# Work at the seams between head pairs moved, and VectorE's remainders ahead of its biased scores

## The reference, cut to what matters

```python
q, k, v = (c.reshape(bsz, seq, 8, 64) for c in (c_q, c_k, c_v))
logf = log_sigmoid(c_f + b_forget);  cum = cumsum(logf, axis=1)
for i in range(8):                        # blocks of 128 queries
    s = q[block i] @ k[:end].T * scale + cum[block i] - cum[:end]   # causal
    p = softmax(s);  o[block i] = p @ v[:end]
y_c = (o * silu(c_gate)) @ p_c
y_m = (softmax(m_q @ mk.T * scale) @ mv * silu(m_gate)) @ p_m
merged = sum_i sigmoid(g_i) * y_i         # i = A, B, C, M
x = layer_norm(alpha * x + merged @ w_out)
```

## Time and profile before

| | us |
|---|---|
| median of 3 runs | 1241.01 (1240.44 to 1241.07) |
| the profiled execution's own time | 1239.63 |
| its span | 1237.8 |
| TensorE busy | 1207.7 (98%) |
| VectorE busy | 800.5 (65%) |
| ScalarE busy | 538.4 (43%) |
| POOL busy | 636.5 (51%) |

### The profile page before, as it was taken

The page is one execution under the profiler, slowest core; times in us unless marked ns, Lnnn a source line. Parts: engine busy times, 40 slices in busy tenths (PEclk is TensorE's granted clock), DMA queues, the critical chain, the costliest instruction groups (busy, mean ns, idle before and its releaser), DMA issues.

```text
span 1237.8 us, 16499 instructions
## 1 busy us (share of the span) xinstructions
PE 1207.7 (98%) x5704; PEld 999.1 (81%) x5704; DVE 800.5 (65%) x1318; ACT 538.4 (43%) x991; POOL 636.5 (51%) x518
## 2 busy tenths in 40 slices
PE   8999999999999999999999999999999999999997
PEld 6888888888888888888788878778787888778886
DVE  5623865676665855347696766677666786876755
ACT  5433424344434444565354555545555443415000
POOL 6687787877876877867122322323312225547000
PEclk9999999999999999999999999999999999999999
DMA  8022131132232332336221111111002533377231
GB/s 274 2 67 69 34 102 51 67 122 104 101 136 102 102 125 86 130 104 200 73 69 52 35 34 51 34 51 51 18 18 86 177 121 115 107 238 249 66 136 68
DMA packets 91268, 118.49 MB, mean 96 GB/s; under 512 B 6072, under 2 KB 72632, under 8 KB 91200
## 3 DMA queue, kind: packets, MB, share of 16 engines
q1 hardware_dynamic: 91200, 117.60, 29.0%
HBM read 92.39 MB, written 25.20 MB: 95 GB/s over the span
## 4 chain that ended last, share of the span: by engine, by line
PE 85%; DVE 8%; issue 3%; ACT 2%; POOL 1%; DMA 1%; DVEq 0%; SPq 0%; ACTq 0%; POOLq 0%
PE pj L744 11%; PE pj L746 11%; PE pj L745 11%; PE pj L816 4%; PE pj L815 4%; PE pj L817 4%; PE pj L1067 4%; PE pt L746 3%; PE pt L744 3%; PE pt L745 3%; PE po L928 2%; PE pj L832 2%; PE pj L834 2%; PE pj L833 2%; PE pt L915 2%
## 5 line engine op out<-in xcount | busy, mean ns | idle before, releaser
L1560 POOL TENSOR_TENSOR ring_lo<-w_pair,ring_hi 128x512 fp32r<-128x512 f32 x168 | 232.3, 1385 | 112.1 <-ACT ring_hi L1123 111.9
L1613 POOL TENSOR_TENSOR w_lo<-w_raw,w_hi 128x128 fp32r<-128x128 f32 (+1 forms) x104 | 108.7, 1063 | 215.1 <-ACT w_hi L1213 213.0
L1123 ACT ACTIVATE ring_hi<-w_pair 128x512 fp32r<-128x512 f32 x168 | 105.1, 628 | 160.6 <-PE pj L746 108.6
L1756 DVE SCALAR_TENSOR_TENSOR po<-glu,cwa,po 128x512 f32<-128x512 f32 x232 | 159.5, 749 | 20.6 <-ACT po L1174 20.6
L744 PE MATMUL pj<-t_hi,ring_hi 128*128 128x512 f32 x392 | 152.8, 390 | 0.3 <-DVE slot L1720 0.3
L746 PE MATMUL pj<-t_hi,ring_lo 128*128 128x512 f32 x392 | 152.5, 389 | 0.0
L745 PE MATMUL pj<-t_lo,ring_hi 128*128 128x512 f32 x392 | 152.5, 389 | 0.0
L815 PE MATMUL pj<-xT_hi,w_hi 128*128 128x512 f32 x320 | 126.4, 395 | 0.0
L816 PE MATMUL pj<-xT_lo,w_hi 128*128 128x512 f32 x320 | 125.5, 392 | 0.0
L817 PE MATMUL pj<-xT_hi,w_lo 128*128 128x512 f32 x320 | 125.0, 391 | 0.0
L1720 DVE TENSOR_TENSOR slot<-pj,copy_p 128x512 f32<-128x512 f32 x56 | 38.6, 689 | 85.6 <-PE pj L746 85.4
(11 more groups left out here) (343 smaller groups left out, 2927.8 us busy)
## 6 DMA issues: line engine op xcount, KB each, us to landing
w_pair<-in_w_in SPq DMA_DIRECT2D x28, 1024.0 KB, 5.2
gate_scratch<-slot SPq DMA_DIRECT2D x16, 1024.0 KB, 4.0
gate<-gate_scratch SPq DMA_DIRECT2D x32, 512.0 KB, 3.7
w_raw<-in_w_in SPq DMA_DIRECT2D x20, 512.0 KB, 3.9
z_scratch<-slot SPq DMA_DIRECT2D x8, 512.0 KB, 2.6
bias<-cum_scratch SPq DMA_DIRECT2D x8, 512.0 KB, 3.7
wout_raw<-in_w_out SPq DMA_DIRECT2D x8, 512.0 KB, 6.2
x_tok<-in_x SPq DMA_DIRECT2D x8, 512.0 KB, 4.2
```

The lines of the kernel that those rows point to most:

```text
L1123: nc.scalar.activation(ring_hi[:, j % RING, :, :], w_src(u, p), ACT.Copy).then_inc(s_rhi, 1)
L1560: nc.gpsimd.tensor_tensor(ring_lo[:, j % RING, :, :], w_src(u, p), ring_hi[:, j % RING, :, :], ALU.subtract).then_inc(s_rlo, 1)
L1613: nc.gpsimd.tensor_tensor(w_lo[:, j % 2, k, :], w_raw[:, j % 2, k, :], w_hi[:, j % 2, k, :], ALU.subtract).then_inc(s_wlo, 1)
L1756: nc.vector.scalar_tensor_tensor(out=acc if n < PAD_A else src, in0=src, scalar=cwa[:, ct, n:n + 1], in1=acc, op0=ALU.mult, op1=ALU.add).t ...
```

## The change

Four edits, none of which changes what is computed.

1. TensorE: the last weighing of a pair (`weigh(c, 7)`) moves behind the first part of the stream in unit 0 of the next pair, and for the last pair behind the first `m_fill` of the memory part. `turn_v` moves from the head of a pair to unit 1, behind the stream's first part, with the two banks of `pt` in swapped order. The last memory weighing moves behind the first half tile of the projection of C. The turning of `mem` is done in two halves with half a tile of stream between them.
2. ScalarE, VectorE and POOL: their counterparts follow. The move and addition of the last output half stand in iteration 1 of the next pair; the copy and remainder of v stand there too, behind `exp` on ScalarE and `biased` on VectorE; POOL's product of z stands in iteration 2, behind the mask addition.
3. VectorE: in each iteration k, `turned_lo(c, k - 1)` stands ahead of `biased(c, k + 1)`, where it was behind it.
4. The four loops over pairs (TensorE, ScalarE, POOL, VectorE) and the one of SP are written out, and three semaphore increments that nobody waits for are gone.

```diff
@@ tensor: weighing, turning of v
-                if n >= 2:
+                if c or n >= 2:
                     pe.wait_ge(s_oadd, PV_PAIR * c + n - 1)
...
-                pe.wait_ge(s_pjfree, 8 * c + 6)
+                pe.wait_ge(s_pjfree, 8 * c + 4 if c else 6)
                 for b in range(2):
+                    if c or b:
+                        pe.wait_ge(s_tlo, TB_PAIR * c + b)
...
             def pair(c, last):
                 s = 4 * c
-                turn_v(c)
                 for u in range(UNITS):
                     cut = 4 * u + (3 if u == 0 else 2)
                     stream_part(s + S_C, S_C, 4 * u, cut)
+                    if u == 0 and c:
+                        weigh(c - 1, UNITS // 2 - 1)
+                    if u == 1:
+                        turn_v(c)
                     turn(c, u)
                     if u + 2 < UNITS or not last:
                         scores(c, u + 2)
                     stream_part(s + S_C, S_C, cut, 4 * u + 4)
                     if u % 2 == 0 and u:
                         weigh(c, u // 2 - 1)
-                weigh(c, UNITS // 2 - 1)
...
+            turn_mem(0)
             pe.wait_ge(s_xfree[1], NP // 2 - 1)
-            stream_tile(1, 1, back=None, halves=range(1, 2))
-            pe.wait_ge(s_mte, n)
+            k_steps(1, 1, 1, 0, KT // 2, 3)
+            turn_mem(1)
+            k_steps(1, 1, 1, KT // 2, KT, 3)
+            pe.wait_ge(s_mte, 2 * MT)
...
             for w in range(2 * NT):
                 m_fill(PER * w, PER * w + 5)
+                if w == 0:
+                    weigh(CT - 1, UNITS // 2 - 1)
...
-            mweigh(NT - 1)
-
             for s in range(S_P + IN_M, S_END):
...
                     p_steps(s, h, 0, p_k(s), 2 * ((s + 1) % 2) + h)
+                    if s == S_P + IN_M and h == 0:
+                        mweigh(NT - 1)
@@ scalar
                 for k in range(UNITS):
+                    if k == 1 and c:
+                        out_shift(1, UNITS // 2 - 1, PV_PAIR * c - 1)
                     if k:
                         turned_hi(c, k - 1)
                         if k + 1 < UNITS or not last:
                             exp(c, k + 1)
+                    if k == 1:
+                        for b in range(2):
+                            act.wait_ge(s_tb, TB_PAIR * c + b + 2)
+                            nc.scalar.activation(v_stack[...], pt[:, 1 - b, :]..., ACT.Copy).then_inc(s_thi, 1)
@@ gpsimd
+                    if k == 2 and c:
+                        z_product(c - 1)
@@ vector
                 if u >= 2:
-                    dve.wait_ge(s_tb, tb + tb_before(u - 1))
+                    dve.wait_ge(s_tb, tb + tb_done(u - 2))
...
                 for k in range(1, UNITS):
+                    turned_lo(c, k - 1)
                     if k + 1 < UNITS or not last:
                         biased(c, k + 1)
-                    turned_lo(c, k - 1)
+                    if k == 1:
+                        for b in range(2):
+                            dve.wait_ge(s_thi, TB_PAIR * c + b + 2)
+                            nc.vector.tensor_tensor(v_stack[...], pt[:, 1 - b, :]..., ...).then_inc(s_tlo, 1)
                     if k + 1 < UNITS or not last:
                         normalise(c, k + 1)
+                    if k == 1 and c:
+                        out_add(1, UNITS // 2 - 1, zc(UNITS // 2 - 1, c - 1), PV_PAIR * c - 1)
...
             mmax(0)
             mnormalise(0)
+            out_add(1, UNITS // 2 - 1, z_raw[:, CT - 1, T - 2 * P:T], PV - 1)
@@ all five engines
-            with pe.Fori(0, CT - 1) as c:
-                pair(c, False)
-            pair(CT - 1, True)
+            for c in range(CT):
+                pair(c, c == CT - 1)
```

## The result

The changed kernel takes 1268.68 us (median of 6 runs, 1267.22 to 1269.64), the kernel before, beside it on the same chip, 1240.57 (6 runs). The ratio is 1.0225, 95% interval 1.0214 to 1.0236: 28.1 us slower, where 1267 was forecast. The profiled execution took 1267.22 us with a span of 1265.4; before it was 1239.63 and 1237.8. It is the fastest of the six, at a mean granted clock of 0.996 where the other five show 0.994 or 0.995.

A forecast was written before the change was run, and what follows sets the result against it. TensorE was taken to bound the kernel. VectorE's order (+34.6 us), the seams (-8.9) and the turning of mem (+0.4) summed to +26.1, said as 1267 us for the median, with an 8 in 10 range of 1248 to 1280.

The forecast's parts named there:

- VectorE's order: In the four pairs: remainder ahead of biased scores makes TensorE's scores wait, 34.6 us slower, bounds 17 to 44.
- odd units: In each pair: remainder plus biased scores end after TensorE wants the banks, 4.3 us lost per pair.
- The removed counters: Semaphore increments taken out, together with the loops written out: priced at 0.
- Units 1 and 2: Where v is turned: late transposes of unit 1 (0.35) and scores of unit 4 (0.75), 1.1 us per pair.
- Even units: In each pair, without units 1 and 2: VectorE comes late from the odd iteration before, 3.5 us lost per pair.
- The seams: Between pairs and around the memory part: moved steps cover TensorE's waits, 8.9 us gained, bounds 6.6 and 9.8.
- the moved weighing: Last pair's end and memory part: stream steps and this weighing cover TensorE's waits, 1.9 of 2.2 us gained.
- The turning of `mem`: Ahead of the first scores: two halves with stream steps between, net 0.4 us slower, bounds -0.7 and +1.1.
- (a): Rival: the order on VectorE costs nothing and only the seams count, 1232 us, chance 0.06.
- (b): Rival: only the odd units pay, as VectorE catches up in the even ones, 1249 us, chance 0.12.
- (d): Rival: the gains and losses cancel, 1241 us, chance 0.02.
- (c): Rival: more stalls than counted, from POOL's product beside VectorE and from written-out code, 1276 us at most, chance 0.14.

The follow-up runs named there:

- e1: The changed kernel with VectorE's old order again, biased scores of unit k+1 ahead of the remainder of unit k-1: 1236.65 us.
- e4: The changed kernel, with VectorE taking the remainder first only in even iterations k and the biased scores first in odd ones: 1238.66 us.
- e8: The changed kernel with the weighing of each even unit directly behind the scores, ahead of the second part of the stream: 1246.92 us.
- e9: The changed kernel with two increments that nobody waits for put back in front of VectorE's two biased-score instructions: 1276.17 us.
- e5: The changed kernel with the first weight split of a pair, on ScalarE and POOL, moved behind the copies of v in iteration 1: 1266.92 us.
- e7: e1 with the last pair's last weighing, its move and addition back where they were, ahead of the memory part: 1235.26 us.
- e2: The kernel before with its five loops over pairs written out and nothing else: 1241.18 us.
- e6: e1 with the turning of mem in one go, as before the change: 1235.10 us.

## Why the prediction was right, and where it was off

**VectorE's order.** Right in its mechanism, and near in its size: 31.3 us measured, 34.6 forecast. e1, e4 and e8 show it from three sides: the cost goes with the order (32.0), with the odd iterations (30.0 of these), and in part, about 14, with an earlier weighing. The odd units came to 3.7 us a pair where 4.3 was forecast, and unit 5, forecast at 1.11, to 0.92; units 11 and 13 came to 1.09 and 0.70 where 0.87 and 0.9 stood. The looped pair spans 83.4 us, as forecast. Of the other signs, the stall at the seam's weighing is gone, and the wait for the biased scores is there, 26 times in the list, six or seven a pair where twelve were named; ten of a pair's units from 3 on are later by over 0.1 us. The longest are units 11 (1.09) and 5 (0.92), not 5 and 13.

**The removed counters.** Priced at 0, which failed. In the changed kernel their absence saves 7.5 us (e9), as it shortens the biased scores by 0.15 us in a unit; I had taken those from the earlier trace rows with the gap inside them. With the counters in place the terms that I put under the order would have come to some 39 us, an estimate (31.3 and 7.5), where 34.6 stood. That the measured 31.3 is near the forecast is in part luck: 34.6 was too low for biased scores with the gap inside, and their getting shorter hid it.

**Units 1 and 2.** The step that failed by its size: 1.1 forecast, 2.6 measured. I had put the stall at unit 1's transposes at 0.35 and it is 2.28. I followed the remainder of v behind the biased scores and the exponential of unit 2, but not those behind the copy `pT_hi` of unit 0, which stands behind a k half (1.06) and two weight splits (1.16) on ScalarE. In the old order VectorE ran the biased scores ahead of that remainder, and in the new one it waits with them. Half of the stall isn't the order's at all: e1, with the old order, has 1.15 in every pair, and the first pair has no more than that in the changed kernel either. e5 shows that this list makes the stall, and also that undoing it alone gives nothing back.

**Even units.** 3.5 forecast without units 1 and 2, 2.4 measured. Unit 4 came to 0.07 where +0.4 stood, unit 6 to 0.25 and unit 8 to 0.35 where 0.65 and 0.6 stood. Units 12 and 14 came to 0.90 and 0.52 where 1.2 and 0.65 stood, but unit 10, put at 0, to 0.29. e9 shows the counters' part: with them back, each of these units is 0.15 later. That leaves 0.1 to 0.25 in each of the others, and 0.44 the other way in unit 10, without an explanation.

**The seams.** The seams between pairs gave 4.9 us of the 5.5 forecast. The end of the last pair and of the memory part gave 1.35 of 3.4: the 1.9 for the moved weighing was wrong in sign, since ScalarE's wait for it delays `za_hi`; e7 shows a loss of 1.4, 0.3 by matmul starts. There I had named the cover on TensorE and not what stands behind the moved instruction on ScalarE, the same omission as in unit 1. The last memory weighing gave 2.3 by matmul starts, its upper bound of 2.25, where 1.5 was taken; it wasn't tried alone. And between the pairs what went at the seam came back for the most part at unit 1, as told.

**The turning of `mem`.** +0.75 against +0.4, within its bounds, with the half clock behind it on top.

**The rivals.** (a), 1232, falls with e1: the order costs. (b), 1249, falls with the trace, in which the even units pay 2.4 us a pair; e4 shows that they do so only once the odd ones do. (d) falls with the result. (c), 1276, had two parts. Written-out code costs nothing here (e2). The POOL part came the other way round: beside POOL's product of z the q remainder was not held, and the product was.

```profile
738.82 1.22 DVE L2050 TENSOR_TENSOR q_stack<-q_raw,q_stack 64x1024 fp32r<-64x1024 f32 x1
738.86 3.42 POOL L1668 TENSOR_TENSOR z_raw<-z_raw,sg 128x1024 f32<-128x1024 f32 x1 [2.64 <-DVE z_raw L2038]
```

VectorE's instruction took 1.22 us, as long as its twin does with POOL idle, and POOL's 3.42 in place of some 2.4. Nobody waits for POOL there, so it cost nothing. In the pairs of instructions that I looked at, the one that started later paid more: VectorE's q remainder started 0.04 us ahead of POOL's product here, and its instruction of the earlier trace rows 0.68 behind one. The kernel before has a third case at the same seam, beside a mask addition of POOL's:

```profile
729.48 1.37 DVE L2039 TENSOR_TENSOR q_stack<-q_raw,q_stack 64x1024 fp32r<-64x1024 f32 x1
729.73 1.44 POOL L1637 TENSOR_TENSOR bdiag<-bias,maskc 128x128 f32<-128x128 f32 x1
```

The addition takes 0.46 by itself, and the q remainder 1.22. This hold of 0.15 on VectorE isn't there after the change. The Trainium skill, Advanced Engine Details and Errata, section GPSIMD Details, says that the two engines conflict for instructions of two SBUF inputs; the trace agrees that there is a conflict, and shows that here POOL paid nearly all of it.

The sum came nearer than its terms. I had 3.3 too much for the order; against that stand 2.1 of gain that the memory part didn't give, 2.9 of half clock, 0.9 at the seams and the turning, and the start's -1.1.

## What to carry to other kernels

In a list that an engine works off in order, an instruction that still hangs on the bounding engine must not stand ahead of one that this engine waits for next; ask first which of the two inputs comes later, not which consumer complains by name. The wait that a profile names (`pT_lo`) may be cured at its source, here by letting the weighing that frees the buffer run 0.7 us sooner, which gave 7.7 us where the reordering lost 32. And when a step is moved, read what stands behind it in the list of every engine that it touches, not only what covers it on the busiest one.

## What the runs showed of the hardware

**An increment between a wait and its instruction has a price.** 0.15 us between two dependent instructions of VectorE, as shown above; on the path it made 7.5 us of a kernel. An increment between instructions that don't depend on each other was not tried.

**A wait in a dense stream can cost more than itself.** In the changed kernel the first scores start 2.82 us late, and a few matmuls on TensorE drops to its half clock: 512-column matmuls follow one another by 0.43 us where it is 0.23. The wait, two matmuls at the lower clock, and the windows before it and in it (columns as above):

```profile
642.79 0.39 PE L899 MATMUL pj<-k_stack_hi,q_stack 128*128 128x256 f32 x1 [2.66 <-DVE k_stack_lo L2056]
644.06 0.62 PE L816 MATMUL pj<-xT_lo,w_hi 128*128 128x512 f32 x1
644.48 0.63 PE L817 MATMUL pj<-xT_hi,w_lo 128*128 128x512 f32 x1
```

```profile
638.00:646.00 8.00, 5.34 (x21) 4.09 (x20) 7.03 (x17) 5.32 (x8) 5.04 (x5) 0.88 0.52 164
646.00:648.00 2.00, 2.00 (x8) 1.57 (x8) 0.32 (x1) 0.00 (x0) 0.00 (x0) 0.63 0.81 233
```

The granted clock is 0.63 of full speed in these 2 us (part of them at 1.2 GHz, the rest at 2.4), and the stretch costs 1.7 us. Another such stretch, in the third pair at 822 to 825, costs 1.25. In e6, where nothing stalls at the first scores, the first one isn't there. But e5 waits as long as the changed kernel at its first scores (bracket 2.6) and goes on at full clock, 1.00 from 640 to 650, and so do e4 and e7. Over the fourteen traces, from 30 to 1200 us, two matmuls of TensorE start 2.0 us or more apart 29 times. Beside 15 of these stands a stretch at half clock, beside 14 none, and none stands anywhere else. What decides was not tried. It makes differences of one to three microseconds between two kernels with such waits uncertain, e6's and e7's among them.
